# Front of a transformer block with experts: x by token tile, first weights in two parts, first products feature by feature

## The reference, cut to what matters

```python
h = rmsnorm(x, attn_norm_g[layer])
qa, ka, va, qb, fb, ib, og, qc, gate_pre = split_cols(h @ w_in[layer], IN_SPLITS)
...
yb = hgrn2_branch(qb, fb, ib, og, lower_bounds[layer], out_norm_b[layer])
yc = memory_branch(qc, rmsnorm(mem, mem_norm_g[layer]), w_mem_kv[layer], q_norm_c[layer], k_norm_c[layer])
```

## Time and profile before

| | us |
|---|---|
| three runs | 1193.73, 1195.39, 1195.55 (median 1195.39) |
| the profiled execution, its own time | 1194.13 |
| its span | 1192.3 |
| PE busy | 1108.4 (93%) |
| DVE busy | 900.0 (75%) |
| ACT busy | 725.9 (61%) |
| POOL busy | 213.9 (18%) |

### The profile page before, as it was taken

The page is one execution under the profiler, slowest core; times in us unless marked ns, Lnnn a source line. Parts: engine busy times, 40 slices in busy tenths (PEclk is TensorE's granted clock), DMA queues, the critical chain, the costliest instruction groups (busy, mean ns, idle before and its releaser), DMA issues.

```text
span 1192.3 us, 16219 instructions
## 1 busy us (share of the span) xinstructions
PE 1108.4 (93%) x5731; PEld 844.5 (71%) x5731; DVE 900.0 (75%) x1123; ACT 725.9 (61%) x926; POOL 213.9 (18%) x145
## 2 busy tenths in 40 slices
PE   4899998999999999998999999999999999999992
PEld 3699987878887787755766666666666666666661
DVE  4486468555444875797999999999989889998881
ACT  7543343334445223316888888888788888888780
POOL 2000000000000000001332442222332333243221
PEclk9999999999999999999999999999999999999997
DMA  5413232221222433647999999999999999999982
GB/s 210 149 54 105 90 98 71 71 71 36 69 71 72 172 106 106 280 181 274 365 358 362 371 370 365 362 363 366 366 369 369 374 367 373 369 372 366 364 289 34
DMA packets 74496, 285.60 MB, mean 240 GB/s; under 512 B 10868, under 2 KB 33416, under 8 KB 49620
## 3 DMA queue, kind: packets, MB, share of 16 engines
q1 hardware_dynamic: 59716, 251.16, 56.0%
q0 software_dynamic: 14736, 33.87, 11.9%
HBM read 272.39 MB, written 29.38 MB: 253 GB/s over the span
## 4 chain that ended last, share of the span: by engine, by line
DMA 47%; PE 39%; DVE 6%; issue 5%; ACT 2%; POOL 0%; SPq 0%; POOLq 0%; DVEq 0%
DMA out_dram<-arena 46%; PE bank L1486 31%; PE bank L1685 1%; PE bank L1663 1%; PE bank L1566 1%; PE bank L1819 1%; PE bank L1675 1%; DMA arena<-in_x_dram 1%; ACT front_split L554 1%; DVE front_split L904 1%; DVE low L1390 1%; DVE front_split L1124 0%; DVE hT_low L910 0%; DMA arena<-in_w_in_dram 0%; DVE lo_hot L1352 0%
## 5 line engine op out<-in xcount | busy, mean ns | idle before, releaser
L1390 DVE TENSOR_TENSOR low<-arena,high 128x2048 fp32r<-128x2048 f32 x192 | 435.6, 2288 | 50.3 <-ACT high L554 48.4
L554 ACT ACTIVATE high<-arena 128x2048 fp32r<-128x2048 f32 x192 | 364.3, 1917 | 37.1 <-DMA arena<-in_w_exp_up_dram 36.4
L1486 PE MATMUL bank<-high,gatheredT 128*96 128x512 f32 x1024 | 326.0, 399 | 20.3 <-DVE gatheredT L1397 13.6
L1486 PEld LDWEIGHTS bank<-high,gatheredT 128*96 128x96 f32 x1024 | 160.6, 162 | 95.1 <-issue 25.6
L1486 PE MATMUL bank<-low,gatheredT 128*96 128x512 f32 x512 | 202.4, 395 | 0.0
L516 POOL DMA_INDIRECT arena<-u_rows,arena x64 | 87.7, 1370 | 578.0 <-DVE arena L1385 526.3
L524 POOL DMA_INDIRECT out_dram<-arena x64 | 120.2, 1878 | 385.3 <-DMA out_dram<-arena 360.9
L554 ACT ACTIVATE arena<-bank 96x512 f32<-96x512 f32 (+4 forms) x217 | 107.8, 534 | 103.2 <-PE bank L1675 51.6
L1486 PE MATMUL bank<-high,hidT 128*96 128x512 f32 x512 | 163.6, 400 | 1.5 <-ACT arena L554 1.5
L1486 PE MATMUL bank<-hT_high,front_split 128*128 128x512 f32 x448 | 143.9, 402 | 4.0 <-DVE front_split L1124 3.2
L1486 PEld LDWEIGHTS bank<-low,gatheredT 128*96 128x96 f32 x512 | 83.0, 162 | 36.4
(11 more groups left out here) (253 smaller groups left out, 1366.7 us busy)
## 6 DMA issues: line engine op xcount, KB each, us to landing
arena<-in_w_exp_up_dram SPq DMA_DIRECT2D x128, 1024.0 KB
arena<-in_w_exp_down_dram SPq DMA_DIRECT2D x64, 1024.0 KB
arena<-in_w_in_dram SPq DMA_DIRECT2D x14, 1024.0 KB, 5.5
arena<-in_w_in_dram SPq DMA_DIRECT2D x10, 768.0 KB, 4.5
arena<-in_w_branches_dram SPq DMA_DIRECT2D x4, 1024.0 KB, 5.0
arena<-in_w_out_dram SPq DMA_DIRECT2D x4, 1024.0 KB, 5.0
arena<-in_x_dram SPq DMA_DIRECT2D x4, 512.0 KB, 5.4
arena<-in_w_mem_kv_dram SPq DMA_DIRECT2D x2, 1024.0 KB, 5.0
```

Of the source, the lines that this page charges most:

```text
L554: return nc.scalar.activation(o, i, ACT.Copy, **kw)
L1390: v.tensor_tensor(low_part[q % SLOTS], raw[q % SLOTS], high_part[q % HIGHS].bitcast(F32), ALU.subtract).then_inc(low_done, 1)
L1486: ins = mm(bank, left[a], right[b], start=first and q == 0, stop=last and q == 2)
```

## The change

- SP: the identity goes by itself behind x tile 0 and the gains' rows go ahead of x tile 3; the wait for x is gone. Block 0 goes in two halves of two k (`first_in` for the first, `front_in[0]` for the second), then the rest of square, mem and block 1.
- ACT: a root of one element ahead of x; per x tile the square and its root. High part of the first half block, feature 0, high part of the second half, the table copies, features 1 to 7, block 1.
- DVE: per tile a reciprocal and the scaling; then low parts: first half block, feature 0, second half, features 1 to 7, the three lb instructions, block 1.
- PE: features 0 to 3 are transposed per token tile; the gains' transpose stands ahead of the last tile's. Behind it the table products, which now wait for the rest of square. Group 0 has its own function: for each k of the first half the four column tiles, one bank each, and behind each k the transposes of feature 4 + k. Then block 1 as before.

```diff
@@ -359,10 +360,12 @@
         def _(sp):
             for t in range(NT):
                 sp.dma_start(x_tok[:, t, :], io["x"][0, t * P:(t + 1) * P, :]).then_inc(x_in[t], 16)
-            for name, r0 in (("attn_norm_g", 0), ("mem_norm_g", 8), ("lb_logits", 20)):
-                src = io[name].rearrange("a (k p) -> (a k) p", p=P)
-                sp.dma_start(gain_rows[r0:r0 + src.shape[0], :], src).then_inc(c_in[2], 16)
-            sp.dma_start(square[:, :, :], const["square"]).then_inc(c_in[0], 16)
+                if t == 0:
+                    sp.dma_start(ident, const["square"][:, 0, :]).then_inc(ident_in, 16)
+                elif t == 2:
+                    for name, r0 in (("attn_norm_g", 0), ("mem_norm_g", 8), ("lb_logits", 20)):
+                        src = io[name].rearrange("a (k p) -> (a k) p", p=P)
+                        sp.dma_start(gain_rows[r0:r0 + src.shape[0], :], src).then_inc(c_in[2], 16)
             w_in = io["w_in"][0].rearrange("(k p) n -> p k n", p=P)
             w_kv = io["w_mem_kv"][0].rearrange("(k p) n -> p k n", p=P)
             w_branch = io["w_branches"].rearrange("(k p) n -> p k n", p=P)
...
@@ -388,8 +391,11 @@
                     src = w_sup[:, 4 * (w - S0):4 * (w - S0) + 4, :]
                 sp.dma_start(raw_block(w), src).then_inc(front_in[w % 2], 16)
 
-            sp.wait_ge(x_in[NT - 1], 16)
-            load_block(0)
+            first_src = w_in[:, 0:2, groups[0][1]:groups[0][1] + groups[0][2]]
+            sp.dma_start(raw_block(0)[:, 0:2, :], first_src).then_inc(first_in, 16)
+            second_src = w_in[:, 2:4, groups[0][1]:groups[0][1] + groups[0][2]]
+            sp.dma_start(raw_block(0)[:, 2:4, :], second_src).then_inc(front_in[0], 16)
+            sp.dma_start(square[:, 1:, :], const["square"][:, 1:, :]).then_inc(c_in[0], 16)
             sp.dma_start(mem[:, :, :], io["mem"][0].rearrange("(t p) d -> p t d", p=P)).then_inc(mem_in, 16)
             load_block(1)
 
...
@@ -562,17 +568,19 @@
                 act.wait_ge(front_in[w % 2], 16 * (w // 2 + 1))
                 copy(split_block(w)[0], raw_block(w)).then_inc(front_high, 1)
 
+            act.wait_ge(c_in[8], 2)
+            nc.scalar.activation(small[:, 318:319], eps, ACT.Sqrt)
             for t in range(NT):
                 act.wait_ge(x_in[t], 16)
                 nc.scalar.activation(xn[:, t, :], x_tok[:, t, :], ACT.Square,
                                      accum_out=small[:, t:t + 1]).then_inc(x_squared, 1)
-            act.wait_ge(c_in[8], 2)
-            act.wait_ge(x_squared, NT)
-            nc.scalar.activation(small[:, 6:10], small[:, 0:4], ACT.Sqrt, bias=eps,
-                                 scale=1.0 / D).then_inc(x_rooted, 1)
+                act.wait_ge(x_squared, t + 1)
+                nc.scalar.activation(small[:, 6 + t:7 + t], small[:, t:t + 1], ACT.Sqrt, bias=eps,
+                                     scale=1.0 / D).then_inc(x_rooted, 1)
             act.wait_ge(gains_done, 1)
             copy(gains[:, 0:24], ps[3][:, 0:24]).then_inc(gains_out, 1)
-            high_block(0)
+            act.wait_ge(first_in, 16)
+            copy(split_block(0)[0][:, 0:2, :], raw_block(0)[:, 0:2, :]).then_inc(first_high, 1)
             act.wait_ge(gains_out, 1)
 
             def feature_major(f):
...
@@ -581,12 +589,15 @@
                 dst, src = (hT[0][:, f, :], ps[4 + f % 4][:, :]) if f < KD else (memT[0][:, f - KD, :], ps[4 + f % 4][:, 0:M])
                 copy(dst, src, scale=gains[:, f:f + 1]).then_inc(f_high, 1)
 
-            for f in range(KD):
-                feature_major(f)
-            high_block(1)
+            feature_major(0)
+            act.wait_ge(front_in[0], 16)
+            copy(split_block(0)[0][:, 2:4, :], raw_block(0)[:, 2:4, :]).then_inc(front_high, 1)
             for k in range(2):
                 act.wait_ge(unit_done, k + 1)
                 copy(table[0:6, k * T:min(SPAN, (k + 1) * T)], ps[k][0:6, 0:min(T, SPAN - k * T)]).then_inc(unit_out, 1)
+            for f in range(1, KD):
+                feature_major(f)
+            high_block(1)
             act.wait_ge(lb_in_exp, 1)
             nc.scalar.activation(lb[:, 0:4], lb[:, 0:4], ACT.Exp).then_inc(lb_exp, 1)
             act.wait_ge(mem_in, 16)
...
@@ -911,18 +922,26 @@
                                        parts[0][:, k, :].bitcast(F32), ALU.mult, ALU.subtract).then_inc(f_low, 1)
 
 
-            dve.wait_ge(x_rooted, 1)
-            then(v.reciprocal(small[:, 12:16], small[:, 6:10]))
             for t in range(NT):
+                dve.wait_ge(x_rooted, t + 1)
+                then(v.reciprocal(small[:, 12 + t:13 + t], small[:, 6 + t:7 + t]))
                 v.tensor_scalar(xn[:, t, :], x_tok[:, t, :], small[:, 12 + t:13 + t], None, ALU.mult).then_inc(x_normed, 1)
 
+            def first_low_part(k0):
+                high_part, low_part = (part[:, k0:k0 + 2, :] for part in split_block(0))
+                return v.tensor_tensor(low_part, raw_block(0)[:, k0:k0 + 2, :], high_part.bitcast(F32), ALU.subtract)
+
+            dve.wait_ge(first_high, 1)
+            first_low_part(0).then_inc(first_low, 1)
+            feature_major(0)
+            dve.wait_ge(front_high, 1)
+            first_low_part(2).then_inc(front_low, 1)
+            for f in range(1, KD):
+                feature_major(f)
             dve.wait_ge(gains_out, 1)
             then(v.tensor_tensor(lb[:, 4:6], gains[:, 20:22], gains[:, 22:24], ALU.max))
             then(v.tensor_tensor(lb[:, 0:2], gains[:, 20:22], lb[:, 4:6], ALU.subtract))
             v.tensor_tensor(lb[:, 2:4], gains[:, 22:24], lb[:, 4:6], ALU.subtract).then_inc(lb_in_exp, 1)
-            low_block(0)
-            for f in range(KD):
-                feature_major(f)
             low_block(1)
 
             for column in (16, 18):
...
@@ -1512,36 +1531,71 @@
                                 pe.wait_ge(gains_out, 1)
                         for kk in range(4):
                             k = 4 * kh + kk
-                            if g == 0:
-                                left, right = [w[:, kk, t * P:(t + 1) * P] for w in weights], [part[:, k, :] for part in hT]
-                            else:
-                                left = [part[:, k, t * P:(t + 1) * P] for part in (memT if name == "kv" else hT)]
-                                right = [w[:, kk, :] for w in weights]
+                            left = [part[:, k, t * P:(t + 1) * P] for part in (memT if name == "kv" else hT)]
+                            right = [w[:, kk, :] for w in weights]
                             last = products(bank[:, 0:width], left, right, k == 0, k == KD - 1)
                         if kh == 1:
                             last.then_inc(unit_done, 1)
                     if kh == 0:
                         last.then_inc(front_used, 1)
 
-            pe.wait_ge(c_in[0], 16)
+            def first_group(n):
+
+
+                weights = split_block(0)
+                for k in range(4):
+                    pe.wait_ge(f_low, k + 1)
+                    if k == 0:
+                        pe.wait_ge(first_low, 1)
+                    elif k == 2:
+                        pe.wait_ge(front_low, 1)
+                    for t in range(NT):
+                        if k == 0 and n + t >= 4:
+                            pe.wait_ge(unit_out, n + t - 3)
+                        last = products(ps[(n + t) % 4][:, :], [w[:, k, t * P:(t + 1) * P] for w in weights],
+                                        [part[:, k, :] for part in hT], k == 0, False)
+                    if k == 3:
+                        last.then_inc(front_used, 1)
+                    feature_major(4 + k)
+                weights = split_block(1)
+                pe.wait_ge(front_low, 2)
+                for t in range(NT):
+                    for kk in range(4):
+                        if t == 0:
+                            pe.wait_ge(f_low, 4 + kk + 1)
+                        last = products(ps[(n + t) % 4][:, :], [w[:, kk, t * P:(t + 1) * P] for w in weights],
+                                        [part[:, 4 + kk, :] for part in hT], False, kk == 3)
+                    last.then_inc(unit_done, 1)
+
+            pe.wait_ge(ident_in, 16)
+
+            def early_features(t):
+                pe.wait_ge(x_normed, t + 1)
+                for f in range(4):
+                    last = tr(ps[4 + f][:, t * P:(t + 1) * P], xn[:, t, f * P:(f + 1) * P], ident)
+                    if t == NT - 1:
+                        last.then_inc(f_done, 1)
+
+            for t in range(NT - 1):
+                early_features(t)
             pe.wait_ge(c_in[1], 16 * 8)
             pe.wait_ge(c_in[2], 16 * 3)
 
             tr(ps[3][:, 0:24], gain_rows[0:24, :], ident[0:24, 0:24]).then_inc(gains_done, 1)
-            pe.wait_ge(x_normed, NT)
-            for f in range(KD):
-                feature_major(f)
+            early_features(NT - 1)
             pe.wait_ge(c_in[5], 16)
             pe.wait_ge(c_in[6], 16)
```

(10 more changed lines are left out.)

3 lines of the change are left out of this document (2 added, 1 removed).

## The result

| | before | after |
|---|---|---|
| median, us (7 runs each) | 1195.09 (1192.7 to 1196.36) | 1201.22 (1197.53 to 1202.8) |
| ratio after / before | | 1.0049 (95% interval 1.0036 to 1.0062) |
| profiled execution, span | 1194.13, 1192.3 | 1201.22, 1199.4 |
| last product of group 0 ends | 46.6 | 52.5 |

The changed kernel is slower, by 6.1 us between the medians. The forecast was 1194.7, with 1192.0 to 1197.7 as its range: the time is outside it, on the side that had a chance of 0.10. One run of e3 further down (1388.89 us, at a granted clock of 0.75 in place of 0.98 and more) is left out of its median and ratio.

A forecast was written before the change was run, and what follows sets the result against it. The prediction took the end of group 0 on PE to set the time: -8.9 + 0.4 + 2.1 + 4.9 + 1.5 = 0.0 us, so 1194.7 + 0.0 = 1194.7 us, range 1192.0 to 1197.7.

The forecast's parts named there:

- start of group 0: First product of group 0 on PE: to start at 15.6 in place of 24.51, 8.9 us earlier.
- clock in the first k: First half of group 0: 0.7 us of products at half rate before PE's full clock near 16.3, costing +0.4 us.
- 16 transposes: Features 4 to 7, four transposes behind each k of group 0's first half: +2.1 us, with a 0.1 allowance per switch.
- pause: PE idle between group 0's halves, 29.0 to 33.9, until block 1's low part, which follows feature 7: +4.9 us.
- clock behind the pause: Products behind the pause at half rate after PE idles: between 0 and 1.9 us, taken as +1.5.
- "13.5" for square: Time in us at which the rest of square, awaited by PE's table products, was to land.
- 64 KB at about 420 GB/s is 0.16 us: Cost of ident's transfer ahead of x tile 1, putting x tile 3 there at about 9.9.
- 1.2 MB at 0.42 MB/us is 2.9 us: Time after 9.5 us for the remaining transfers up to square, with about 1 us more added.
- Rival 3: Slower: square lands late and holds the table products; at 200 GB/s it lands at 16.5, +3.0, 1197.7; 9% with rival 4.
- Rival 1: PE's clock holds through the pause ahead of block 1: -1.5 us, 1193.2; chance 14%.
- rival 2: Pause is short, feature 7's copies and block 1 running beside k = 3 products: 1188.3; 7% with other gains.
- Rival 4: Group 0 not early because first_in or feature 0 is late; low part at 18 gives 1197.1; 9% with rival 3.

The follow-up runs named there:

- e3: Changed kernel, but PE waits for square only at the first bias product, not at the table products; ratio to before 1.0028, median 2.7 us above before's.
- e5: Changed kernel with the 64 KB of ident issued behind x tile 3 instead of tile 0; ratio to before 1.0021, median 2.5 us above before's.
- e10: Changed kernel with 44 more, never read transposes on PE in the pause ahead of block 1; ratio to before 1.0025, median 3.0 us above before's.
- e1: Changed kernel with block 1 split on ACT and DVE behind feature 3, ahead of features 4 to 7; ratio to before 0.9978, median 2.6 us below before's.
- e7: Changed kernel with the edits of e1 and e3 together; ratio to before 0.9967, median 3.5 us below before's.
- e8: e7 with e5's edit added, ident behind x tile 3; ratio to before 0.9968, median 3.9 us below before's.
- e9: e8 with POOL's out_norm alone also waiting for x tile 3; ratio to before 0.9961, median 4.4 us below before's.
- e4: Changed kernel with POOL issuing bucket and out_norm behind x tile 3; ratio to before 1.0054, median 5.5 us above before's.
- e6: Changed kernel with the three small gains rows issued behind x tile 3; ratio to before 1.0049, median 5.9 us above before's.
- e2: Changed kernel with SP's wait for x tile 3 put back ahead of the first weights; ratio to before 1.0057, median 6.9 us above before's.

## Why the prediction was wrong, point by point

| term | predicted | measured | how |
|---|---|---|---|
| start of group 0 | -8.9 | -5.2 | 19.27 against 24.51 |
| clock in the first k | +0.4 | +2.1 | 4.84 against 2.74 |
| 16 transposes | +2.1 | +1.8 | four times 0.44 |
| pause | +4.9 | +4.9 | 34.16 to 39.05 |
| clock behind the pause | +1.5 | +2.3 | 13.24 for 48 products (39.05 to 52.29) against 10.94 |
| sum | 0.0 | +5.9 | |

**The step that failed** is "13.5" for square, and within it "64 KB at about 420 GB/s is 0.16 us" and "1.2 MB at 0.42 MB/us is 2.9 us". It is 3.7 of the 5.9 us: 3.2 for square (16.74 against 13.5), the rest for the hand-over and the table products (2.29 against 2.1). The prediction took transfers for a stream in order in which bytes count at 420 GB/s, with 1 us on top. The strips show otherwise (GB/s, half a us per number, 0 to 20 us; first after, then e5):

```profile
GB/s 0 0 0 106 131 369 374 277 259 254 262 336 279 224 190 353 385 353 379 398 399 388 309 266 240 355 386 426 420 413 412 427 399 393 397 389 377 205 127 98
```

```profile
GB/s 0 0 0 106 246 418 426 377 410 205 148 295 313 354 363 340 327 343 385 395 405 299 253 218 327 350 440 394 443 415 410 393 406 414 397 385 358 98 25 12
```

Two readings. First, with ident behind tile 0 the stream falls to 277 to 254 GB/s between 3.5 and 5 us, where e5 moves 377 to 410 until 4.5: by 10 us after has moved 2.46 MB, e5 2.73 (the other runs 2.42 to 2.65 with ident there, 2.64 and 2.84 with it behind x). Tile 3, by the prediction there at 9.9, was squared at 11.41. In after that is hidden behind square; in e3 it binds. Second, and larger: everything up to square is 3.8 MB, and the first 28 numbers of after's strip, that is 14.0 us, already hold that much. But square landed at 16.7, when 5.0 MB had moved. So more than a megabyte of the transfers issued behind square (mem and block 1, at 6.80 and 7.55) had moved before it counted as landed; that is 2.8 us. In e5 the 3.8 MB are full at about 13.4 and square lands at 14.98: 1.6 us. The prediction had the 3.8 MB at 12.4 and 1 us for the landing. So in after about half of the error is the rate (13.9 against 12.4) and half the landing (2.8 us against 1.0). The landing is also what varies: with the very transfers of after it was 1.1 us behind the bytes in e10 (15.04) and 3.1 in e1 (17.27), while the bytes were full at 14.0 and 14.2. So that ident's place made square land sooner in e5 isn't shown.
The Trainium skill, "DMA: Bandwidth & Descriptors", "Queues, rings and completion order", says that one copy is split over up to 16 rings, one on each DMA engine, and that the copies of one issuing engine need not complete in the order of issue. By that rule the counts above agree. No view here tells the engines apart, so which of them lagged, and why so small a transfer makes them lag, isn't shown.

Rival 3 named the right place, the constant that the table products wait for, and the right price: "to be slower by 2.4 us square has to land at 15.9". It landed at 16.7. Its dip to 200 GB/s did not come (224 and 190 for one us, 350 on the mean from 9.5 to 14); a smaller loss of rate and a late landing did it together. What it had wrong was the chance, put low because the rate looked safe. A wait put into PE's queue for a tensor that isn't needed there (e3) should have been counted with a range for its landing, not at the mean rate.

**The clock ahead of the pause** was undersized by 1.7 us. The mechanism was named; what failed is "steady work now starts at 12.5, so full rate comes near 16.3". In after PE works from 12.09 to 15.04 with 0.49 us idle, then waits for 1.94 ahead of the table products, and full rate is back at about 23.5. The wait is not the whole cause: in e3 and e7 the table products follow the transposes without a wait and still take 2.2, and the first 12 products 4.23 and 5.08 where the prediction had 3.1. Transposes that come tile by tile, with waits for x between them, did not bring the full rate in time in any of these runs; twelve in one piece did (e8: the table products at 12.96 take 1.24). Yet such a start did not come free either: in e5, e8 and e9 PE waits for 0.9 to 1.4 us ahead of the table products or of group 0, the granted clock goes back to 0.50, and the first 12 products take 4.54, 4.62 and 4.55.
On whether transposes count, runs now say more than the trace did. Twelve transposes and four more brought the table products of e5 to full rate, and 44 held it through e10's pause. The Trainium skill, "TensorE: Matmul & The Clock Gate", Part 4, says that they don't; by that rule both would have run at half rate, and the measurement decides against it here.

**The transposes** cost 0.44 for four, without the allowance of 0.1. **The pause** came out within 0.02 us, as the same path of copy, high part and low part; it was read off the order of the instructions and the durations in before. **The clock behind it** came at 2.3 (2.2 by e10), above the 1.9 that I had set as its bound from a wait of another length in another stretch. Rival 1 (the clock holds) falls; rival 2 needs another order on ACT, as was said, and e1 is that order: without the pause the same change is faster. Rival 4's input, the low part of feature 0, did not bind the start in after, and stands right ahead of it in e8 and e9.

The premises held: the end of group 0 sets the time, later work is covered, and the sum is 0.0 only because a gain of 8.9 was to pay for costs of 8.9. A sum of large terms of both signs should have had a wider range on the slower side, as its one gain rested on the least known number. How much of the 5.9 is the start depends on the execution read (17.58 in e10, 19.80 in e1 for the same front); the one read here is at least the median of its seven runs.

Two things stay open. The end of group 0 in e1 is 1.0 us earlier than before and its bias products take 1.6 us more, so by the chain it should be 0.6 us later than before; measured is 2.6 less, with an interval that reaches down to 0.6 us (0.9995). Some 2.2 of that gap of 3.2 us is the choice of executions: before's profiled one (1194.13) is 2.0 us below the median of before in that session (1196.13), e1's (1193.77) 0.2 above its own. The last us is open. So is why ident's place matters so much beyond its bytes.

## What to carry to other kernels

Work that is started earlier is only worth what its latest input allows: take from the trace when each transfer has landed, the constants too, and give a landing that starts a chain a range (here square came 1.1 to 3.1 us behind its bytes). Wait for a tensor where it is read, not ahead of work that does not read it (e3). When an order on PE is interleaved more finely, look at what the other engines now get later (here the last feature, and behind it the weights of the second half), and move the independent work ahead of the dependent work in their queues: that order (e1) was worth 7 us at the end of group 0, more than the whole change cost. A pause on PE can cost more than its length: here 4.9 us, and another 2.2 to 2.3 in half-rate products.

## What the runs showed of the hardware that was not expected

- 64 KB issued between x tiles 0 and 1 made tile 1 2.8 us later (8.21 against 5.36 in e5 and 5.39 in before; 7.35 to 8.73 over the executions with this order); the same bytes behind tile 3 did not.
- With POOL's bucket and out_norm, 275 KB on the other queue, held back, tile 1 came at 6.61 (e4); with out_norm alone held back x came no sooner (e9).
- A constant issued ahead of two transfers of 1 MB landed 1.1, 2.8 and 3.1 us after the bytes up to it had moved (e10, after, e1), in kernels whose transfers are the same.
- The bias products behind a wait of 2.3 us took 1.98 or 1.99 in before, after, e3 to e6 and e10, 3.04 in e9, and 3.53 to 3.63 in e1, e2, e7 and e8. The granted clock sorts them: over the first 2 us of these products it was 1.00 in the seven quick ones, 0.50 in e1, e2 and e8, 0.57 in e7 and 0.70 in e9. What made it fall in these five isn't shown. The wait and PE's work ahead of it are alike. All seven quick ones start between 55.50 and 61.38, all others ahead of 54.5 or at 62.99; that may be chance. It takes 1.5 us from a gain, or doesn't.
- Unread transposes in a pause hold the full rate of what follows (e10: 11.19 against 13.42 for 48 products).
